# Spreading the rows of 16-row diagonal blocks by two rounded products instead of one full fp32 product

## What is computed

```python
def chunk_gated_delta_rule(q, k, v, g, beta):
    ...
    g = jnp.cumsum(g, axis=-1)
    decay = jnp.exp(jnp.where(causal, g[..., :, None] - g[..., None, :], -jnp.inf))
    m = jnp.where(strict, jnp.einsum("bhnid,bhnjd->bhnij", k_beta, k) * decay, 0.0)
    a_mat = jnp.eye(CHUNK, dtype=q.dtype) + m
    u = lax.linalg.triangular_solve(a_mat, v_beta, left_side=True, lower=True)
    w = lax.linalg.triangular_solve(a_mat, k_beta * jnp.exp(g)[..., None], left_side=True, lower=True)
    ...

def gated_deltanet(h, w_in, conv_w, a_log, dt_bias, norm_w, w_out):
    proj = h @ w_in                                   # 1024 -> 4096 + 16 columns
    qkv = jax.nn.silu(causal_dwconv(qkv, conv_w))     # 4 taps
    ...
    o = chunk_gated_delta_rule(...)
    ...
    return o @ w_out
```

## Time and profile before

| what | value |
|---|---|
| three runs | 1241.79, 1242.69, 1245.47 us; median 1242.69 |
| the profiled execution's own time | 1242.52 us |
| its span in the trace | 1240.7 us |
| mean granted TensorE clock | 0.995 |
| busy: TensorE, its weight loads | 98%, 91% |
| busy: VectorE, ScalarE, GpSimd | 59%, 58%, 71% |
| DMA | 217.76 MB, mean 176 GB/s |

### The profile page before, as it was taken

One profiled execution on the slowest core, in us unless ns is written; L12 is line 12 of the kernel. 1 busy time (PEld: TensorE's weight loads), 2 busy tenths in 40 slices (PEclk: granted clock), 3 DMA queues, 4 the chain that ended last, 5 costly groups with the idle time before them and its releaser, 6 DMA issues.

```text
span 1240.7 us, 26051 instructions
## 1 busy us (share of the span) xinstructions
PE 1219.8 (98%) x9010; PEld 1124.2 (91%) x9010; DVE 735.6 (59%) x1720; ACT 722.5 (58%) x1327; POOL 880.1 (71%) x387
## 2 busy tenths in 40 slices
PE   9999999999999999999999999999999999999997
PEld 3688899988998889899999999999999999999986
DVE  3989972244587774159884375555635757555633
ACT  3656654565666665469642366665655547666743
POOL 0357857569869888958533258888898868888795
PEclk9999999999999999999998999999999999999999
DMA  9995354446546665645332136555566555655562
GB/s 370 408 368 186 102 188 153 120 147 206 180 145 207 188 191 162 193 144 162 119 94 79 52 94 194 177 180 174 164 186 190 180 161 172 196 176 185 156 199 70
DMA packets 66038, 217.76 MB, mean 176 GB/s; under 512 B 9904, under 2 KB 17328, under 8 KB 62624
## 3 DMA queue, kind: packets, MB, share of 16 engines
q1 hardware_dynamic: 65952, 216.59, 54.4%
HBM read 215.52 MB, written 1.05 MB: 175 GB/s over the span
## 4 chain that ended last, share of the span: by engine, by line
issue 38%; POOL 37%; PE 22%; ACT 1%; POOLq 1%; DVE 1%; ACTq 0%; DVEq 0%
POOL w_lo L673 37%; PE bank L802 10%; PE bank L1135 5%; PE bank L894 3%; PE bank L903 1%; PE bank L898 1%; POOL w_lo L680 1%; POOLq L670 0%; ACT h L1689 0%; ACT w_hi L1689 0%; POOLq L672 0%; PE bank L724 0%; PE bank L948 0%; PE bank L729 0%; PE bank L725 0%
## 5 line engine op out<-in xcount | busy, mean ns | idle before, releaser
L673 POOL TENSOR_TENSOR w_lo<-w_raw,w_hi 128x1024 fp32r<-128x1024 f32 x340 | 812.6, 2403 | 322.8 <-ACT w_hi L1689 321.6
L1689 ACT ACTIVATE w_hi<-w_raw 128x1024 fp32r<-128x1024 f32 (+1 forms) x372 | 378.1, 1020 | 103.0 <-PE bank L903 35.8
L802 PE MATMUL bank<-a_hi,w_hi 128*128 128x264 f32 (+3 forms) x704 | 200.6, 285 | 0.6 <-DVE a_lo L3674 0.6
L802 PE MATMUL bank<-a_hi,w_lo 128*128 128x264 f32 (+3 forms) x704 | 200.4, 285 | 0.0
L802 PE MATMUL bank<-a_lo,w_hi 128*128 128x264 f32 (+3 forms) x704 | 200.1, 284 | 0.0
L802 PEld LDWEIGHTS bank<-a_hi,w_hi 128*128 128x128 f32 x704 | 133.0, 189 | 0.8 <-DVE a_lo L3674 0.8
L802 PEld LDWEIGHTS bank<-a_lo,w_hi 128*128 128x128 f32 x704 | 133.0, 189 | 0.1
L802 PEld LDWEIGHTS bank<-a_hi,w_lo 128*128 128x128 f32 x704 | 133.0, 189 | 0.0
L3749 DVE SCALAR_TENSOR_TENSOR bank<-row_mean,cols,bank 128x260 f32<-128x260 f32 (+3 forms) x112 | 54.6, 487 | 116.5 <-ACT cols L1689 113.8
L763 PE MATMUL bank<-a_parts,w_hi 128*128 128x256 f32 x448 | 81.5, 285 | 0.5 <-DVE a_parts L2952 0.4
L894 PE MATMUL bank<-g_parts,w_hi 128*128 128x512 f32 x308 | 79.0, 397 | 0.0
(11 more groups left out here) (549 smaller groups left out, 2926.9 us busy)
## 6 DMA issues: line engine op xcount, KB each, us to landing
w_raw<-in_s SPq DMA_DIRECT2D x284, 512.0 KB, 3.6
w_raw<-in_down SPq DMA_DIRECT2D x48, 512.0 KB, 3.5
adaw<-in_w_ada SPq DMA_DIRECT2D x16, 1024.0 KB, 10.3
w_raw<-in_down SPq DMA_DIRECT2D x24, 384.0 KB, 3.1
adab<-in_w_ada_first SPq DMA_DIRECT2D x8, 1024.0 KB, 8.8
ctxt<-in_ctx SPq DMA_DIRECT2D x1, 1024.0 KB, 11.3
x<-in_x SPq DMA_DIRECT2D x1, 1024.0 KB, 15.3
out_h<-h SPq DMA_DIRECT2D x4, 256.0 KB, 2.6
```

Of the source, the lines that this page charges most:

```text
L673: pool.tensor_tensor(w_lo[:, s], w_raw[:, s], w_hi[:, s].bitcast(F32), ALU.subtract) \
L802: ins = mm(banks[bank][:, tk], w_[:, s, k], x_[:, k, tk], start=(m == 0), stop=(m == 3 * KD - 1))
L1689: return nc.scalar.activation(out_, in_, f, **kw)
```

## The change

`spread_rows()` takes two fp32r matmuls for each k instead of one fp32 matmul. `pick16`, all zeros and ones, becomes fp32r. The values are split into a rounded part `diag_hi` and a remainder `diag_lo`, both fp32r, both laid out with the 24 lanes innermost (`[128, 16, 24]`, so that the moving operand `diag_hi[:, k+1:]` is one contiguous piece). The products are added up in PSUM. The spread rows therefore come out with the lanes innermost too, and `eliminate` reads them through a turned view.

The split is made by two engines. For chunks 1 and 2 ScalarE writes `diag_hi[:, :, 0:16]` in place of `diag16`, and does it ahead of `rounded(12)`, `activated(11)` and `squared(11)` instead of behind them; VectorE subtracts it from bank 4 into `diag_lo`. For chunk 0 VectorE copies `diag16` to `diag_hi` and subtracts. `diag16` shrinks to chunk 0. `spread_ready` counts to 3 (`pick16` and the two subtractions) instead of 2.

```diff
-        pick16 = at("pick16", [P, BLOCK - 1, P], area_a + 17536)
+        pick16 = at("pick16", [P, BLOCK - 1, P], area_a + 17536, F32R)
-        diag16 = at("diag16", [P, 3 * HN, BLOCK], arena + 41984)
+        diag16 = at("diag16", [P, HN, BLOCK], arena + 41984)
+        diag_hi = at("diag_hi", [P, BLOCK, 3 * HN], arena + 54272, F32R)
+        diag_lo = at("diag_lo", [P, BLOCK, 3 * HN], arena + 55808, F32R)
...
             def spread_rows():
-                pe.wait_ge(spread_ready, 2)
+                pe.wait_ge(spread_ready, 3)
...
-                        dst = banks[BANKS[name][0]][:, o_:o_ + 3 * HN * n].rearrange("p (a n) -> p a n", n=n)
-                        ins = mm(dst, pick16[:, k], diag16[:, :, k + 1:], start=True, stop=True)
+                        dst = banks[BANKS[name][0]][:, o_:o_ + 3 * HN * n].rearrange("p (n a) -> p n a", n=n)
+                        mm(dst, pick16[:, k], diag_hi[:, k + 1:], start=True, stop=False)
+                        ins = mm(dst, pick16[:, k], diag_lo[:, k + 1:], start=False, stop=True)
...
             tap3(12)
+            act.wait_ge(stage_done, DONE["cd"])
+            fn(diag_hi[:, :, 0:2 * HN].rearrange("p i a -> p a i"), banks[4][:, 0:2 * P].rearrange("p (a i) -> p a i", i=BLOCK), ACT.Copy).then_inc(taken[4], 1)
             rounded(12)
             activated(11)
             squared(11)
-            act.wait_ge(stage_done, DONE["cd"])
-            fn(diag16[:, 0:2 * HN], banks[4][:, 0:2 * P].rearrange("p (a i) -> p a i", i=BLOCK), ACT.Copy).then_inc(taken[4], 1)
...
-                        dst = src[:, i] if c else diag16[0:cn, 2 * HN + hh]
+                        dst = src[:, i] if c else diag16[0:cn, hh]
...
-                v.memset(diag16[:, 2 * HN:], 0.0).then_inc(spread_ready, 1)
+                v.memset(diag16[:], 0.0)
...
-                    row = spread[list(SPREAD).index(name)][:, o_:o_ + 3 * HN * n].rearrange("p (a n) -> p a n", n=n)
+                    row = spread[list(SPREAD).index(name)][:, o_:o_ + 3 * HN * n].rearrange("p (n a) -> p a n", n=n)
...
             key_products(0, 3)
-            taps(11, 12, 13)
+            dve.wait_ge(taken[5], TURN["kk0", 5] + 1)
+            link(v.tensor_copy(diag_hi[:, :, 2 * HN:], diag16[:].rearrange("p a i -> p i a")))
+            v.tensor_tensor(diag_lo[:, :, 2 * HN:], diag16[:].rearrange("p a i -> p i a"), diag_hi[:, :, 2 * HN:].bitcast(F32), ALU.subtract).then_inc(spread_ready, 1)
+            taps(11, 12)
+            dve.wait_ge(taken[4], TURN["cd", 4] + 1)
+            v.tensor_tensor(diag_lo[:, :, 0:2 * HN], banks[4][:, 0:2 * P].rearrange("p (a i) -> p i a", i=BLOCK),
+                            diag_hi[:, :, 0:2 * HN].bitcast(F32), ALU.subtract).then_inc(spread_ready, 1)
+            taps(13)
             eliminate(0, 7)
```

## The result

The changed kernel takes 1245.51 us (median of 12 runs, 1244.22 to 1247.92), the one before, beside it, 1243.33 (median of 12 runs, 1241.79 to 1245.47). The ratio is **1.0019, with an interval from 1.0011 to 1.0027**: slower by 2.2 us. Forecast were 0.25 us less: the time lies inside the range given, the direction was wrong. I had taken 0.3% for what a measurement can tell from no change; twelve runs on either side told 0.08%. Measured twice more, each time beside the kernel before, the same kernel came out at 1.0033 (1.0021 to 1.0045) and 1.0024 (1.0014 to 1.0033).

The account below looks back on a forecast made before the run. TensorE, busy 98% of the span, was taken as the bound. Products 1.8 us shorter, less a 1.3 us wait, end the spread 0.65 earlier; VectorE's clock leaves 0.25: 1242.4 us from median 1242.69, range 1240.4 to 1246.3.

Parts of the forecast that it names:

- What becomes of the gain: After the spread: VectorE's elimination and list run as before, TensorE meets its clock at `fI1`/`kq1`; 0.2 to 0.3 us left.
- The case: Rival, chance 0.19: elimination's turned reads, 96 bytes apart, slow VectorE and the kernel; 1244.8 us at 0.73 ns more per element.
- Its dearer form: Turned reads in the elimination at double cost, 1.04 ns more per element: TensorE 3.1 us late, 1245.8 us.
- the pair of reductions: Profile rows summing 128 elements on VectorE: 368 ns at 64 bytes, 275 contiguous; taken as upper reading for turned reads.
- The products: Spread on TensorE: rounded part and remainder take 3.8 us against 5.6, 1.8 us less, with a floor of about 0.118 us each.
- The wait ahead of them: TensorE before the spread's products waits for VectorE's last subtraction: a new wait of 1.3 us, bounds 0 and 1.7.
- The end of the spread: TensorE, held at most 0.05 us for ScalarE's bank copies, ends the spread at 601.5 against 602.17: 0.65 us gained.
- Where the wait would show: Sign in the profile after: a new TensorE wait of 0.4 us in `fI1` or `kq1`, ended by VectorE.
- The clock: TensorE's granted clock stays up behind the new wait ahead of the spread's products; nothing charged.
- Costed at nothing: ScalarE's moved copy, GpSimd's remainder starting at 594.9 instead of 593.89, and `pick16` in fp32r were charged nothing.

Follow-up runs that it names:

- the turned kernel: Kernel before, with only its full fp32 products writing rows heads innermost and VectorE's elimination reading them turned, 96 bytes apart; 1.0019 of the kernel before.
- the early-remainder kernel: Changed kernel with VectorE taking the second remainder ahead of the taps of tiles 11 and 12; 1.0016 of the kernel before.

## Why the prediction was wrong

The step that failed is the one under "What becomes of the gain": "VectorE starts the elimination when it started before ... Then its list goes on as before". It starts within 0.04 us of the time given. But its 15 multiplications read SBUF with 96 bytes between neighbours and take 3.2 us more in sum, 1.1 ns for each of the 2880 elements. The case was on the list, with a chance of 0.19. Its dearer form (1.04 ns an element, 3.1 us on TensorE, 1245.8 us) is the case that happened. That the median, 1245.51, came so close to its time is in part luck: the list makes TensorE 2.6 us late at `kq1`, not 3.1 (A and B of the turned kernel, 163.60 against 161.05), the falls of the clock, charged with nothing, come on top, and the median of the kernel before is 1243.33 over twelve runs, not 1242.69.

Why the chance was too low can be said too. I read the pair of reductions, 0.73 ns more for each element at 64 bytes, as an upper value, because their outputs could explain the gap as well. Measured by itself, 64 bytes costs (714 - 504)/336 = 0.63 ns: the row was near the price, not an upper end. And at 96 bytes it is (952 - 504)/336 = 1.33.

Point by point:

- *The products.* 3.80 us, as worked out. By pieces it differs: in `sp5`, from 600.50 to 601.36, eight starts are 0.107 us apart, not 0.118.
- *The wait ahead of them.* 1.15 us where 1.3 stood. The clock stayed at 1.00 behind it.
- *The end of the spread.* 0.70 us earlier where 0.65 stood.
- *What becomes of the gain, had VectorE not been slowed.* With contiguous reads 0.7 to 0.8 us are left in the profiles, not 0.2 to 0.3. TensorE does wait 0.29 us for VectorE in `fI1`, but `kq1` then starts at once, where it waited 0.26 us for ScalarE before. And the second half of `kq1` was misplaced: `kq1` and `kq2` are 32 records in 3.84 us, so it began near 621.7 before, not at 621.2, and VectorE's copy, done at 620.85, was no bound for it. That term was too small, and it didn't decide.
- *Where the wait would show.* I put VectorE's delay at the second half of `fI1`. It shows first at `hq`, since the taps of tile 15 stand among the elimination steps and ScalarE's squares hang on them. That place I had not looked at. When `hq` is moved, the wait comes out at `fI1`, so the loss is the same list by another door.
- *The clock.* I charged nothing for waits. The wait ahead of the products kept the clock up; the one of 2.56 us that I did not foresee brought it down, which costs 0.8 us at `kq1`.
- *Costed at nothing.* `pick16` takes 3.60 us as before, and GpSimd's later remainder held nobody. ScalarE's copy of 256 elements went from 0.37 to 0.80 us. It now writes turned and rounds; no run separates the two, but rounding alone takes ScalarE about 1 ns for each element (1024 in 1.05 us), so the turned write is the likely cause. Its cover, the idle time behind it, held.

The profiled executions are 4.9 us apart, and the parts make 4.8: VectorE +3.3 (A); in B, -0.7 because TensorE now waits for VectorE and has nothing to catch up at `kq1`, the fall at `hq` +0.8, the second fall +1.4. The -0.7 is not the shorter products, as I had it in what I expected of the changed kernel's second profile: the turned kernel has it with the long ones. The medians are only 2.2 to 4 us apart. The execution of before that was profiled, 1242.52 us, is among its quick ones, and the second fall, which all three profiles of the changed kernel show, need not come in each execution; how often it comes was not measured.

The version with contiguous reads throughout is the better kernel by its profiles, with A of before and a B that is 0.72 and 0.85 us shorter; its two measurements are 0.9987 and 0.9996, of which only the first excludes no change.

## What to carry to other kernels

A layout that suits one engine is paid for by the next reader of the data: before turning an operand, look for every instruction that walks the result and ask how many bytes lie between neighbours. For VectorE in SBUF, at 336 elements, 8 bytes were free, 16 and more took 1.4 to 1.5 times as long and 96 bytes 1.9 times; PSUM could be read turned at no cost by VectorE and ScalarE, so turn there, or let all tiles of a loop change their layout together. And a delay of an engine with a fixed list comes out first at the earliest instruction that anybody waits for in it, here the taps among the elimination steps, not at its end.

## What the runs showed of the hardware that I had not expected

- VectorE's reading of SBUF at 96 bytes, 952 ns for 336 elements, is dearer than at 64 (714) and at 192 (720). The distance alone doesn't order the prices, and at 96 bytes rows of three elements and fewer cost nothing more (72 elements, 0.23 us either way).
- A turned write of SBUF costs VectorE the same as a turned read (954 ns against 952).
- A TensorE idle time of 2.56 us was followed by a granted clock of 0.50 for some 3 us; an idle time of 1.15 us, in the same kernel, was not followed by any fall. The length of the wait alone doesn't decide: 1.66 us in the early-remainder kernel was followed by a fall, behind narrow products, and 1.72 us in the turned kernel was not.
- A fall of the clock near 640 us, behind products of 64x32 and 32x32, comes in the profiles of some kernels and not of others, once with and once without in the same one, and costs 1.4 us there. It may be part of the scatter of this program; that was not tried.
